# A hybrid block with sixteen experts: the last experts' rows added by matrix products, smaller tiles, earlier refills, and a split last output tile

## What is computed

```python
x = x + g1 * (y @ w_out)
h = rms_norm(x, norm_ffn) * (1 + sc2) + sh2
# router: best of 4 groups, then the 2 best experts of that group
p_group = softmax(h @ w_rg + b_rg)
g_top = argmax(p_group)
p_exp = softmax((h @ w_re + b_re)[group g_top])
pe_top, e_top = top_k(p_exp, 2)
w_e = pe_top / sum(pe_top) * p_group[g_top]
# every expert: D = 1024, F = 512
for e in experts:
    hid = silu(h @ w_gate[e]) * (h @ w_up[e])
    y += (hid * combine[e]) @ w_down[e]
x = x + g2 * y
return rms_norm(x, final_norm)
```

## Time and profile before

| what | value |
|---|---|
| median of 3 runs | 781.9 us (779.35 to 783.69) |
| profiled execution, own time | 781.9 us |
| its span | 780.0 us |
| TensorE busy | 686.8 us, 88% |
| VectorE busy | 318.2 us, 41% |
| ScalarE busy | 180.0 us, 23% |
| GpSimd busy | 116.7 us, 15% |
| moved by DMA | 173.62 MB, 223 GB/s over the span |

### The profile page before, as it was taken

One profiled execution on the slowest core, in us unless ns is written; L12 is line 12 of the kernel. 1 busy time (PEld: TensorE's weight loads), 2 busy tenths in 40 slices (PEclk: granted clock), 3 DMA queues, 4 the chain that ended last, 5 costly groups with the idle time before them and its releaser, 6 DMA issues.

```text
span 780.0 us, 9903 instructions
## 1 busy us (share of the span) xinstructions
PE 686.8 (88%) x3851; PEld 401.5 (51%) x3851; DVE 318.2 (41%) x752; ACT 180.0 (23%) x434; POOL 116.7 (15%) x164
## 2 busy tenths in 40 slices
PE   1799899999999999879999985899999999999830
PEld 1674446667666697545654455444444544443210
DVE  3203657856466533786612228350211211202126
ACT  3204215122121121456711141020111211201103
POOL 8700122313032155000000000010000000000030
PEclk9989999999999999899999986999999999999975
DMA  9999003793330300750085047638999999999965
GB/s 332 375 264 364 3 1 108 245 294 109 108 108 1 52 5 7 266 216 2 1 324 108 28 179 280 195 110 349 375 423 413 405 413 409 390 404 410 421 208 201
DMA packets 75475, 173.62 MB, mean 223 GB/s; under 512 B 21954, under 2 KB 38940, under 8 KB 71836
## 3 DMA queue, kind: packets, MB, share of 16 engines
q1 hardware_dynamic: 69520, 157.59, 56.0%
q0 software_dynamic: 2672, 9.44, 3.5%
q10 hardware_dynamic: 3228, 5.84, 2.0%
HBM read 156.59 MB, written 16.26 MB: 222 GB/s over the span
## 4 chain that ended last, share of the span: by engine, by line
PE 76%; DVE 9%; POOL 4%; issue 4%; ACT 3%; DMA 3%; POOLq 0%; ACTq 0%; DVEq 0%
PE ps L1031 14%; PE ps L1153 7%; PE ps L1064 7%; PE ps L2300 7%; PE ps L2267 5%; PE ps L1025 4%; PE ps L1059 2%; PE ps L2378 2%; PE ps L2264 2%; PE ps L2384 2%; DMA expert_rows<-yo 2%; PE ps L2291 2%; POOL lev L1648 2%; PE ps L653 2%; PE ps L2388 2%
## 5 line engine op out<-in xcount | busy, mean ns | idle before, releaser
L1031 PE MATMUL ps<-gu,xgT 128*128 128x512 f32 x256 | 113.0, 600 | 3.6 <-DVE xgT L1110 2.5
L1031 PEld LDWEIGHTS ps<-gu,xgT 128*128 128x128 f32 x256 | 48.6, 192 | 63.2 <-issue 63.2
L2300 PE MATMUL ps<-hT,winr 128*128 128x512 f32 x144 | 72.6, 612 | 0.0
L1540 POOL DMA_INDIRECT xg<-xn_rows,list x15 | 13.9, 928 | 384.7 <-DVE list L1447 185.9
L1153 PE MATMUL ps<-wout,yT 128*128 128x512 f32 x128 | 57.6, 610 | 0.0
L1064 PE MATMUL ps<-dn,hidT 128*128 128x512 f32 x128 | 56.5, 594 | 0.0
L1753 POOL TENSOR_TENSOR cc<-low,lev 128x512 f32<-128x512 f32 x20 | 30.2, 1518 | 129.5 <-DVE low L2087 104.0
L1891 DVE SCALAR_TENSOR_TENSOR acc<-ada,st,acc 128x512 f32<-128x512 f32 x56 | 48.5, 866 | 1.3
L2267 PE MATMUL ps<-hT,wind 128*128 128x512 f32 x96 | 43.4, 605 | 0.0
L1025 PE MATMUL ps<-gu,xgT 128*32 128x256 f32 (+1 forms) x384 | 43.0, 452 | 0.0
L1153 PEld LDWEIGHTS ps<-wout,yT 128*128 128x128 f32 x128 | 24.6, 195 | 30.0 <-issue 30.0
(11 more groups left out here) (433 smaller groups left out, 1046.6 us busy)
## 6 DMA issues: line engine op xcount, KB each, us to landing
dn<-in_w_down SPq DMA_DIRECT2D x16, 2048.0 KB, 23.3
gu<-in_w_gate SPq DMA_DIRECT2D x15, 2048.0 KB, 21.5
gu<-in_w_up SPq DMA_DIRECT2D x15, 2048.0 KB, 26.0
ada<-in_w_ada SPq DMA_DIRECT2D x12, 2048.0 KB, 11.6
expert_rows<-zero SPq DMA_DIRECT2D x12, 512.0 KB, 6.7
expert_rows<-yo ACTq DMA_DIRECT2D x8, 512.0 KB
wout<-in_w_out SPq DMA_DIRECT2D x1, 3072.0 KB, 10.6
x<-in_x SPq DMA_DIRECT2D x2, 1024.0 KB, 6.2
```

The lines of the kernel that those rows point to most:

```text
L1031: ins = nc.tensor.matmul(PS[2 * b + w][:, :], T["xgT"][:, k, :], w_in[:, w, k, :], start=(k == 0), stop=(k == KT - 1))
L2300: ins = t.matmul(bank[:, :], w(k), T["hT"][:, k, :], start=(k == 0), stop=(k == KT - 1))
```

## The change

It has five parts.

1. **Sizes.** Seven tiles of 128, five of 64, four of 32 rows. The last three places are now 32-row experts, the place before them (`MID`) a 64-row one.
2. **Last three experts on the chip** (`CHIP` = 3). Their rows aren't stored and gathered; DVE writes them into an SBUF tile `yc` of 128 rows, the first 32 of which are zero. A matrix `back`, built by DVE from slots and weights and transposed by TensorE behind the gate product of place 4, says which row goes to which token and with what weight. In `pe_back`, behind the last down product, TensorE sums for each token tile `diag(w1) y1 + diag(w2) y2 + back yc` in PSUM, and DVE adds that to `x2`. Both groups of gathers now wait only for the stores of the places before: the first group for the gate product of place 13 and the store of place 11, the second for the store of place 12. The slots of on-chip rows point to a zeroed row.
3. **Quarter refills** of gate and up for places 4 and 5 too.
4. **Last output tile by column halves**: tile 2's transposes and logits, and the first half of tile 3's, stand between the products of the second half; DVE copies the second half of tile 3's transposes out.
5. **Norms**: the epsilon and the division by 1024 are taken into ACT's root, so that DVE's variance steps go; the code for extra tiles is moved behind the sums and skipped with one branch.

The diff, cut to its core:

```diff
-SIZES = [128] * 8 + [64] * 4 + [32] * 4
+SIZES = [128] * 7 + [64] * 5 + [32] * 4
+CHIP = 3
+ORDER = list(range(NBUF))
+_big, _less = list(range(NBUF, BIG)), list(range(E - CHIP - 1, BIG - 1, -1))
+while _big:
+    ORDER += [_less.pop(0), _big.pop(0)]
+ORDER += _less + list(range(E - CHIP, E))
...
-                if n == NBUF:
+                if n < 2 * NBUF:
+                    b = n - NBUF
                     for part in range(4):
                         if part < 3:
-                            sp.wait_ge(sem("first_gu_mm"), part + 1)
+                            sp.wait_ge(sem("first_gu_mm"), 3 * b + part + 1)
                         else:
-                            sp.wait_ge(sem("gu_mm"), 1)
+                            sp.wait_ge(sem("gu_mm"), b + 1)
...
+    def pe_back(pe):
+        pe.wait_ge(sem("routing"), ROUTING["route_i"])
+        pe.wait_ge(sem("exp_out"), 3)
+        pe.wait_ge(sem("diag"), 1)
+        pe.wait_ge(sem("y1_in"), 16 * ST)
+        for i in range(ST):
+            if i == 2:
+                pe.wait_ge(sem("yo_d"), E + 1)
+            for n in range(2):
+                if n:
+                    pe.wait_ge(sem(f"y_in{i}"), 16)
+                for w in range(2):
+                    nc.tensor.matmul(PS[2 * i + w][:, :], T[f"diag{n + 1}"][:, i, :],
+                                     T[f"y{n + 1}"][:, i, w * 512:(w + 1) * 512], start=(n == 0), stop=False)
+            pe.wait_ge(sem("yo_d"), E + 1)
+            for w in range(2):
+                ins = nc.tensor.matmul(PS[2 * i + w][:, :], T["back"][:, i * P:(i + 1) * P],
+                                       T["yc"][:, w * 512:(w + 1) * 512], start=False, stop=True)
+            ins.then_inc(sem("oproj_mm"), 1)
...
+        if on_chip(n):
+            dve.wait_ge(sem("yo_d"), E - CHIP + 1)
+            dve.wait_ge(sem("xg_tr"), E)
+            to = slice(32 * (n - E + CHIP + 1), 32 * (n - E + CHIP + 2))
+            for w in range(4):
+                rows, c = slice(32 * w, 32 * w + 32), slice(256 * w, 256 * w + 256)
+                ins = nc.vector.tensor_tensor(T["yc"][to, c], PS[down_bank(n)][rows, 0:256], T["g2q"][rows, :],
+                                              ALU.mult)
...
+        output_products(last, Y_ORDER, (0,)).then_inc(sem("oproj_mm"), 1)
+        all_transposes(last - 1)
+        output_products(last, Y_ORDER[:4], (1,))
+        all_logits(last - 1)
+        pe.wait_ge(sem("x2"), last + 1)
+        transposes(last, 0).then_inc(sem("x2_tr"), 1)
+        output_products(last, Y_ORDER[4:], (1,)).then_inc(sem("oproj_mm"), 1)
+        pe.wait_ge(sem("x2T"), 2 * last + 1)
+        logits(last, 0)
+        pe.wait_ge(sem("x2"), last + 2)
+        transposes(last, 1).then_inc(sem("x2_tr"), 1)
+        pe.wait_ge(sem("x2T"), 2 * last + 2)
+        logits(last, 1).then_inc(sem("logit_mm"), 1)
...
+        for i in range(ST):
+            dve.wait_ge(sem("oproj_mm"), ST + 1 + i + 1)
+            for w in range(2):
+                x = T["x2"][:, i, w * 512:(w + 1) * 512]
+                ins = v.tensor_tensor(x, PS[2 * i + w][:, :], x, ALU.add)
+            ins.then_inc(sem("x3"), 1)
...
         pool.wait_ge(sem("routing"), ROUTING["slots"])
-        pool.wait_ge(sem("yo_st"), 16 * STORED[E - 1])
+        pool.wait_ge(sem("gu_mm"), E - CHIP + 1)
+        pool.wait_ge(sem("yo_st"), 16 * STORED[E - CHIP - 1])
         for i in range(ST):
             rows_back(0, "y1_in", i)
-        pool.wait_ge(sem("yo_st"), 16 * STORED[E])
+        pool.wait_ge(sem("yo_st"), 16 * STORED[E - CHIP])
         for i in range(ST):
             rows_back(1, f"y_in{i}", i)
```

More of the change, by code:

```diff
@@ L188, in sbuf_map @@
     o2 = at("r16", o2, [P, ST, E])
+    at("back", o2 + 2 * K, [P, S])
+    at("diag1", o2, [P, ST, P])
     o2 = at("in_row", o2, [P, 2, ST, P])
@@ new lines, in transposes, with logits @@
+        def transposes(w, half):
+            for k in range(4 * half, 4 * half + 4):
+                ins = t.transpose(PS[4 + half][:, (k % 4) * P:(k % 4 + 1) * P], T["x2"][:, w, k * P:(k + 1) * P],
+                                  idf[:])
+            return ins
+        def logits(w, half):
+            lg = PS[7][:, w * 20:w * 20 + 20]
+            for k in range(4 * half, 4 * half + 4):
+                ins = t.matmul(lg, T["x2T"][:, k, :], T["wrA"][:, k, :], start=(k == 0), stop=(k == KT - 1))
+            return ins
@@ new lines, in all_transposes, with all_logits @@
+        def all_transposes(w):
+            pe.wait_ge(sem("x2"), w + 1)
+            if w:
+                pe.wait_ge(sem("x2T"), 2 * w)
+            transposes(w, 0)
+            transposes(w, 1).then_inc(sem("x2_tr"), 1)
+        def all_logits(w):
+            pe.wait_ge(sem("x2T"), 2 * w + 2)
+            pe.wait_ge(sem("wrA"), 1)
+            logits(w, 0)
+            logits(w, 1).then_inc(sem("logit_mm"), 1)
+        pe_output_start(pe).then_inc(sem("oproj_mm"), 1)
+        for k in range(KT):
+            t.matmul(PS[7][:, 80:100], mod[:, 24 + k:25 + k].broadcast_to([P, P]), T["wr"][:, k, :],
+                     start=(k == 0), stop=(k == KT - 1))
@@ L1252, in extra @@
             pe_down(pe, n)
-        extras(pe, extra)
+        extras(pe, n_extra, extra)
     def act_moe(act):
@@ L1689, in _ @@
         link(g.iota(T["row_i"][:], pattern=[[1, P]], base=0, channel_multiplier=0))
-        edges = [0] + STEPS_DOWN + [E - 1, E, E + EXTRA]
-        runs = [(a, b, (SIZES + [P] * EXTRA)[a]) for a, b in zip(edges, edges[1:])]
+        runs, a = [], 0
+        while a < E + EXTRA:
+            b, step = a + 1, max(1, (TILE_START + [0])[a + 1] - TILE_START[a])
+            while b < E + EXTRA and TILE_START[b] - TILE_START[b - 1] == step:
+                b += 1
+            runs.append((a, b, step))
+            a = b
         for a, b, step in runs:
```

271 lines of the change are left out of this document (166 added, 105 removed).

## The result

The changed kernel takes 782.5 us at the median (778.8 to 789.7, 20 runs), the kernel before, timed beside it, 779.4 (774.3 to 783.7, 20 runs). The ratio is 1.005, 95% interval 1.0028 to 1.0073: slower by half a per cent, where the forecast was 3.2 us faster. Timed again later it was 785.9 beside 778.7, ratio 1.0077 (1.0046 to 1.0108). A few runs far slower than the rest of their kernel (one of 854.8 us in e5, one of 1406 us in e13, one of 799 us of the kernel before) are left out of ratios and medians. The profiled execution has its own time at 782.5 and a span of 780.8 us.

The account below looks back on a forecast made before the run. TensorE sets the pace with DMA nearly level; the last weights' landing decides. Last down product ends at 745.7, plus 20.6 + 1.4 + 6.0 + 3.05 = 776.8 against 780.0, -3.2 us: forecast 778.7, range 772.5 to 786.

Parts of the forecast that it names:

- Router's start: Behind the last output tile: router starts 2.3 us earlier, set by DVE's scaling; net -1.9 us for the first expert.
- TensorE in the loop: Expert loop: 10.0 us less TensorE work; place 15, ready early, waits for weights and starts 3.9 us earlier.
- DMA from 575 on: Expert loop: queue empty at about 575, full from 577.15; 66.4 MB at 407 GB/s, last down weights land at 743.1.
- The gathers: Before the last weights: gathers of expert rows move at 63 GB/s from about 711 to 740, taking 1.8 MB.
- the gathers take the weights' place: Rival, before place 15: all 4.2 MB go ahead of the last weights, 5.8 us, 785.4 in the runs' measure; chance 0.2.
- The clock: Place 15: low clock after idle adds 1.7 us; rival, low through the products, 799, or 789 if half; chance 0.07.
- The end: Behind the last down product: 24 matmuls 20.6 us, adds 1.4, final passes 6.0, landing 3.05; worth 1 us.
- Extra tile: Rival, after all experts: eighth expert over 64 tokens needs a 17th tile, over 60 us more, 840; chance 0.01.
- fuller stream: Rival, DMA in the expert loop: 420 GB/s moves the 66.4 MB in 5.0 us less, 773.7; chance 0.24.

Follow-up runs that it names:

- e5: Changed kernel with the quarter refills of places 4 and 5 undone; 786.7 us from five runs, ratio 1.0115.
- e13: The kernel of e3 again, on another chip; 782.0 us, ratio 1.0055.
- e8: Changed kernel with the last output tile whole again, norm steps and DVE's copy kept; 787.5 us from six runs, ratio 1.0116.
- e9: Kernel before with column halves, their norm step and quarter refills added, old end kept; 778.6 us beside 778.7, ratio 0.9974.
- e1: Changed kernel with all eight gathers held until place 15's gate and up weights have landed; 776.8 us, ratio 0.9986.
- e4: Changed kernel with 13 unread matmuls added where TensorE waited for weights, to keep it warm; 783.7 us, ratio 1.0076.
- e12: The changed kernel itself, timed again; 785.9 us, ratio 1.0077.
- e6: Kernel before with only the quarter refills of places 4 and 5 added; 779.1 us beside 778.7, ratio 1.0015.
- e7: Changed kernel with the tile sizes of before (eight of 128, four of 64, four of 32 rows); 780.3 us, ratio 1.0039.
- e15: The kernel of e10 with the gathers held to the end of place 15's gate-and-up product; 771.8 us, ratio 0.993.
- e10: e1 with first choices added by DVE instead of TensorE, on-chip products first, 16 products instead of 24; 781.7 us, ratio 1.002.
- e11: e1 with the tile sizes of before (8, 4, 4); 784.0 us, ratio 1.0058.
- e14: The kernel of e10 again; 779.5 us, ratio 1.0026.
- e3: e1 with products reordered: all first choices, then on-chip rows, then second choices tile by tile; 777.6 us, ratio 0.9988.
- e18: The kernel of e15 again; 770.9 us, ratio 0.9905.
- e2: Changed kernel with only the second four gathers held until place 15's gate and up weights have landed; 779.8 us, ratio 1.0014.

## Why the prediction was wrong

- **Router's start: right.** From T the first gate product comes 3.7 us sooner; 1.7 of that is a slow stretch that the kernel before had in its last output tile and this execution had not. e8 puts the halves at 2.0 us, forecast 2.3 with the norm step. The logits' end (460.3) and DVE's scaling (459.48 to 460.63) lie 0.3 us apart, where the forecast had 0.6, and DVE is the later one, as foretold. What is not shown is that these 2 us reach the end: e9 with them is no faster than before.
- **TensorE in the loop: right.** Its work was ready early: 2.6 and 9.0 us idle before place 15, the second released by the gate-and-up weights.
- **DMA from 575 on: right in kind.** The queue moved 302 GB/s in 570 to 575, then was full; 600 to 700 gave 401 GB/s, forecast 407.
- **The gathers: this term failed.** "At 63 GB/s from about 711 to 740 the gathers take 1.8 MB" came from one store of 0.52 MB beside the weights. They took 4.19 MB, 127 GB/s over 33 us: 2.4 MB more, 5.9 us at 407 GB/s. Taking them away gave 5.7 us (e1; 5.0 by the ratios, 6.9 against e4). It is the rival "the gathers take the weights' place", priced at 5.8 us and given 0.2; I let one row outweigh the turns by packets, and read that row wrongly: while the store's packets were moving it had 104 packets beside 115, and 100 GB/s. The forecast's -3.2 us with 5.9 added is +2.7; measured are +3.1 at the medians.
- **Where the miss lies.** From T the forecast has place 15 at 295.2, its down product at 300.2 and the end at 335.0; measured are 296.5, 306.0 and 341.6, later by 1.3, 5.8 and 6.6 us. So most of it is the landing of the last down weights. (The forecast's three hold the slow stretch of 1.7 us, without which they would be that much earlier and the miss larger; the profile of before was also 2.5 us above its median, so these are not better than to 2 or 3 us.)
- **A slip in the rival.** It says that the gain is gone from 3.5 MB ahead on, near 120 GB/s. By the forecast's own rate 3.2 us are 1.3 MB, so it is gone from 3.1 MB on, near 107 GB/s.
- **The clock: half right.** The granted clock was low again for place 15, and twice, not once: 0.50 in 736 to 741 and again from 746 to 751, behind the wait of 2.19 us for the down weights. The down product took 3.64 instead of 1.93 us as forecast (+1.7), the first tile's products 1.3 more; the gate product's 2.5 more lay under its down weights' landing. e4 took all of it away and the median did not fall.
- **The end: right.** 22.0 us of products (20.6 forecast, the difference being the first tile's clock), then 10.0 to the end of the span (10.45 forecast): 31.9 from the end of the last down product against 31.05, and 32.05 before. So the new end buys nothing by itself: the matmuls take what the gathers and passes took. Other profiles say the same: 30.7 to 30.8 for the new end in e4, e5, e8 and e12, and for the old one 31.0 in e9 and 29.0 in e6, so the old one may even be the shorter.
- **Extra tile, fuller stream:** neither came; e5 to e9 give no proof that quarter refills, sizes or column halves change the time, and no run undoes the on-chip rows or the new norm steps alone.

## What to carry to other kernels

When two DMA queues are both full, count packets, not bytes, and ask of every transfer that a change lets start earlier what it will be in front of: gathers that nobody needed for 25 us and more moved 4.2 MB ahead of weights that TensorE waited for. Read a transfer's rate from the windows in which its packets move, not from its time to landing. An engine that gets faster can let such transfers in earlier, and so win nothing (10 us of TensorE work more in e7 cost nothing). Then look for the balance: e1 moved the wait from weights to rows, and only e15, with the on-chip products first and the first choices given to the idle DVE, turned the freed time into a gain.

## What the runs showed of the hardware that was not expected

A matmul's signal can come late while POOL issues gathers. In e10, e11, e13 and e14 the gate product of place 15 ends in the record at 744.08, 737.55, 735.79 and 738.03 us, POOL's last gather ends at 748.07, 744.04, 740.62 and 742.94, and ScalarE's silu starts at 749.81, 745.82, 742.35 and 744.65: 1.7 to 1.8 us behind POOL's last issue each time, 5.7 to 8.3 behind the product. In e1 and e3, on another chip, the same waits with the same gathers show nothing of it, and e3 and e13 are one program (777.6 and 782.0). With the gathers issued behind that signal it never showed there (e15 to e18); at e15's down product DVE starts 1.1 us late. The changed kernel has it at place 14, where TensorE waits for weights afterwards anyway: the gate product ends at 713.76, POOL's first four gathers at 715.97, and the silu starts at 717.32; e12 has 718.98, 721.17 and 722.52. In e2, e4, e5 and e8, on two other chips, gathers are issued there too, and the silu follows the product within 0.1 us. The kernel before shows something alike: its last down product ends at 747.95, the first four gathers are being issued (746.83 to 751.5), and DVE starts at 750.03, 2.1 us behind; in e9 it is 1.5 us, in e6 0.5. In the changed kernel TensorE's small transposes and the down product of place 13 come in pieces with gaps of 0.3 to 1 us while the first four gathers are issued (711.3 to 716), and in e12 again. That POOL's issues are the cause is what all this fits, not what it shows: what differs between the chips is in no row here.
